# Four and four: the order of the high and low matmuls inside a chunk of a split fp32 projection

## What is computed

```python
proj = jnp.einsum("bsd,de->bse", h, w_in[l])
...
x = x + gate1[:, None, :] * jnp.einsum("bsd,de->bse", merged, w_out[l])
...
ff = jnp.square(jax.nn.relu(jnp.einsum("bsd,df->bsf", h2, w_ff1[l])))
x = x + gate2[:, None, :] * jnp.einsum("bsf,fd->bsd", ff, w_ff2[l])
...
h = jnp.einsum('bsd,dn->bsn', x, w_in)
```

## Time and profile before

| | |
|---|---|
| median of 3 runs | 2717.64 us (2717.5 to 2718.73) |
| span of the profiled execution | 2715.6 us |
| PE busy in it | 2667.7 us, 98% |
| PE weight loads busy | 2305.3 us, 85% |
| DVE busy | 1945.2 us, 72% |
| ACT busy | 1379.7 us, 51% |
| POOL busy | 145.2 us, 5% |

### The profile page before, as it was taken

The page is one execution under the profiler, slowest core; times in us unless marked ns, Lnnn a source line. Parts: engine busy times, 40 slices in busy tenths (PEclk is TensorE's granted clock), DMA queues, the critical chain, the costliest instruction groups (busy, mean ns, idle before and its releaser), DMA issues.

```text
span 2715.6 us, 38672 instructions
## 1 busy us (share of the span) xinstructions
PE 2667.7 (98%) x15098; PEld 2305.3 (85%) x15098; DVE 1945.2 (72%) x2837; ACT 1379.7 (51%) x2049; POOL 145.2 (5%) x179
## 2 busy tenths in 40 slices
PE   7999999999999999999999999999999999999997
PEld 6788788888888888888888888878888888888886
DVE  7776888887898876666666676666566766665666
ACT  2158666554544655445544445545554455445643
POOL 0000000000001000000000010100001121000002
PEclk9999999999999999999999999999999999999998
DMA  9964777778888675665565555665545556655453
GB/s 390 409 224 146 260 238 255 272 270 300 292 321 319 230 243 185 191 190 187 187 193 187 179 182 181 191 181 178 156 160 185 187 181 191 185 181 161 147 173 115
DMA packets 162533, 583.98 MB, mean 215 GB/s; under 512 B 19088, under 2 KB 20368, under 8 KB 162352
## 3 DMA queue, kind: packets, MB, share of 16 engines
q1 hardware_dynamic: 157248, 567.71, 62.3%
q0 software_dynamic: 4528, 12.43, 1.7%
q10 hardware_dynamic: 576, 1.37, 0.1%
HBM read 574.05 MB, written 2.15 MB: 212 GB/s over the span
## 4 chain that ended last, share of the span: by engine, by line
PE 86%; DVE 7%; DMA 3%; ACT 2%; issue 1%; SPq 0%; ACTq 0%; DVEq 0%
PE bank L794 49%; PE bank L802 25%; PE bank L755 3%; DVE both_w L1463 2%; DMA raw<-in_w_x 2%; PE pO L851 1%; PE pS L828 1%; PE bank L760 1%; DMA raw<-in_ada 1%; PE bank L740 1%; ACT both_w L1058 1%; PE pT L840 1%; DVE XC L1926 1%; PE bank L772 1%; PE pS L897 1%
## 5 line engine op out<-in xcount | busy, mean ns | idle before, releaser
L1463 DVE TENSOR_TENSOR both_w<-raw,both_w 128x1024 fp32r<-128x1024 f32 x848 | 1036.7, 1234 | 453.1 <-ACT both_w L1058 448.4
L1058 ACT ACTIVATE both_w<-raw 128x1024 fp32r<-128x1024 f32 x848 | 878.1, 1048 | 517.6 <-PE bank L802 458.3
L794 PE MATMUL bank<-H,both_w 128*128 128x512 f32 x4000 | 1015.7, 396 | 2.6 <-ACT both_w L1058 1.2
L794 PEld LDWEIGHTS bank<-H,both_w 128*128 128x128 f32 x4000 | 721.1, 189 | 144.5 <-issue 6.3
L802 PEld LDWEIGHTS bank<-H,both_w 128*128 128x128 f32 x4000 | 545.5, 190 | 40.7 <-DVE both_w L1463 1.3
L802 PE MATMUL bank<-H,both_w 128*128 128x256 f32 x4000 | 557.5, 282 | 0.9 <-DVE both_w L1463 0.9
L794 PE MATMUL bank<-F,both_w 128*128 128x512 f32 x1024 | 256.4, 392 | 0.0
L1503 DVE SCALAR_TENSOR_TENSOR raw<-raw,CR 128x1024 f32<-128x1024 f32 x192 | 232.5, 1217 | 18.3 <-DMA raw<-in_ada 17.0
L794 PEld LDWEIGHTS bank<-F,both_w 128*128 128x128 f32 x1024 | 184.2, 189 | 32.8
L802 PEld LDWEIGHTS bank<-F,both_w 128*128 128x128 f32 x1024 | 139.7, 190 | 10.0
L802 PE MATMUL bank<-F,both_w 128*128 128x256 f32 x1024 | 142.8, 282 | 0.0
(11 more groups left out here) (293 smaller groups left out, 2523.3 us busy)
## 6 DMA issues: line engine op xcount, KB each, us to landing
raw<-in_w_in SPq DMA_DIRECT2D x360, 512.0 KB, 3.9
raw<-in_w_ff SPq DMA_DIRECT2D x256, 512.0 KB, 3.9
raw<-in_ada SPq DMA_DIRECT2D x192, 512.0 KB, 5.2
raw<-in_w_out SPq DMA_DIRECT2D x96, 512.0 KB, 4.5
raw<-in_w_vw SPq DMA_DIRECT2D x48, 512.0 KB, 3.7
raw<-in_w_x SPq DMA_DIRECT2D x32, 512.0 KB, 15.7
raw<-in_w_lru_out SPq DMA_DIRECT2D x32, 512.0 KB, 4.8
raw<-in_w_attn_out SPq DMA_DIRECT2D x32, 512.0 KB, 5.0
```

Source lines behind the costliest of these rows:

```text
L794: pe.matmul(out[i].rearrange("p (a s) -> p a s", a=2), whi[:, s, at_:at_ + 128], both[:, :, kt, :], start=(c == 0 and k == 0), stop=False, ...
L1058: act.activation(whi[:, s, 0:el.n], raw[el.slot][:, 0:el.n], ACT.Copy).then_inc(s_hi, 1)
L1463: dve.tensor_tensor(wlo[:, s, 0:n], raw[el.slot][:, 0:n], v32(whi[:, s, 0:n]), ALU.subtract).then_inc(s_lo, 1)
```

## The change

In `products_wide` the loop over k is cut in two halves of two k each. Each half does its four wide matmuls and then its four narrow ones: a chunk is 4 wide, 4 narrow, 4 wide, 4 narrow, where it was 8 wide, 8 narrow. The number of matmuls and weight loads, their shapes, the banks, the two waits for the weights and the one signal at the end are as before. The wait for `s_lo` now stands before the fifth matmul of the chunk instead of before the ninth. The sum in a bank is taken in another order. No other function is touched.

```diff
-            for k in range(4):
-                kt = 4 * un.corder[c] + k
...
-            pe.wait_ge(s_lo, split_no[order[ch]])
...
-            for k in range(4):
-                kt = 4 * un.corder[c] + k
...
+            for pair_ in range(2):
+                for k in (2 * pair_, 2 * pair_ + 1):
+                    kt = 4 * un.corder[c] + k
...
+                        pe.matmul(out[i].rearrange("p (a s) -> p a s", a=2), whi[:, s, at_:at_ + 128], both[:, :, kt, :],
+                                  start=(c == 0 and k == 0), stop=False, skip_group_check=True)
+                if pair_ == 0:
+                    pe.wait_ge(s_lo, split_no[order[ch]])
+                for k in (2 * pair_, 2 * pair_ + 1):
+                    kt = 4 * un.corder[c] + k
...
+                        ins = pe.matmul(out[i][:, high], wlo[:, s, at_:at_ + 128], xh[:, kt, :], start=False,
+                                        stop=(c == un.nkc - 1 and k == 3), skip_group_check=True)
```

More of the change, by code:

```diff
@@ L783, in products_wide @@
             out = [banks[un.bank + i] for i in range(2)]
+            high = slice(256, 512) if un.x in ("Y0", "Y1") else slice(0, 256)
             pe.wait_ge(s_hi, split_no[order[ch]])
-            for k in range(4):
-                kt = 4 * un.corder[c] + k
[L787 to L795, removed]
@@ L796, in products_wide @@
-            pe.wait_ge(s_lo, split_no[order[ch]])
-            high = slice(256, 512) if un.x in ("Y0", "Y1") else slice(0, 256)
-            for k in range(4):
-                kt = 4 * un.corder[c] + k
[L800 to L803, removed]
+            for pair_ in range(2):
+                for k in (2 * pair_, 2 * pair_ + 1):
+                    kt = 4 * un.corder[c] + k
+                    if begins[un.x] is un:
+                        pe.wait_ge(*ready[un.x](kt))
+                    elif un.kind == "q" and un.j == 0:
+                        pe.wait_ge(*ready["H1"](kt))
+                    for i in range(2):
+                        at_ = k * 256 + i * 128
+                        pe.matmul(out[i].rearrange("p (a s) -> p a s", a=2), whi[:, s, at_:at_ + 128], both[:, :, kt, :],
[4 more added lines that the diff above has]
+                    kt = 4 * un.corder[c] + k
+                    for i in range(2):
+                        at_ = k * 256 + i * 128
+                        ins = pe.matmul(out[i][:, high], wlo[:, s, at_:at_ + 128], xh[:, kt, :], start=False,
+                                        stop=(c == un.nkc - 1 and k == 3), skip_group_check=True)
```

## The result

| | before | changed |
|---|---|---|
| median, 12 runs each | 2717.39 us | 2722.57 us |
| ratio, 95% interval | | 1.002 (1.0012 to 1.0027) |
| span of the profiled execution | 2715.6 us | 2720.4 us |

What follows compares the result with a forecast made beforehand. PE's pace was taken to bound the kernel. The order added +9.0 us, low-weight wait and fresh activations were entered as 0: span 2724.6 us, plus 2 us between span and median, 2726.6 us; range 2710 to 2734.

Steps and rivals of the forecast that it cites:

- slower: Whole kernel: measured time over 2723.1 us, about 0.2% (5.4 us) above no change; chance 0.60.
- What bounds the kernel: Whole kernel: PE, busy 98% of the span, sets the pace; only its waits and matmul distances can matter.
- The order of wide and narrow: PE's 772 chunks: two full wide-narrow turns instead of one add 11.7 ns a chunk, +9.0 us.
- The wait for the low weights: PE's wait for DVE's low split, four wide matmuls earlier: two chunks lack enough lead, +0.5 to +1.8 us.
- Fresh activations: Two PE standstills, 906.77 and 1646.36: four narrow matmuls fill the idle time, -0.9 us together.
- The reason under the main term: PE's chunks: four narrow matmuls unsettle wide ones as much as eight, since narrow ones settle after two; supports +9.0 us.
- Never settled: PE's chunks: wide matmuls stay unsettled, narrow ones partly offset it; +5 ns a chunk, +4 us, 2722 us; chance 0.12.
- Whole price per turn: PE's chunks: the second turn costs the whole 20 ns; +15.4 us, 2733 us; chance 0.11.
- Faster: PE's chunks: unsettling goes by the number of narrow matmuls just before, so four cost less; 2707 to 2711 us; chance 0.18.
- No change: PE's chunks: two half turns cost one; 2717.6 us, give or take 2; chance 0.15.
- The rule named beside it: PE's matmul distances: N/2.4 + 2.5 ns from column count alone, without memory; 2600 ns a chunk in either order.

Runs made afterwards that it cites:

- wait alone: Kernel before, eight wide and eight narrow kept, only the low-weight wait moved ahead of the fifth wide matmul; 2717.76 us against 2717.27, ratio 1.0002.
- 6, 2, 2, 6: Kernel before with each chunk reordered to 6 wide, 2 narrow, 2 wide, 6 narrow; 2717.45 us in one execution against 2717.35.
- rotated: Kernel before with each chunk reordered to 4 wide, 8 narrow, 4 wide, low-weight wait before the narrow ones; 2717.65 us against 2717.27, ratio 1.0001.
- two and two: Kernel before with each chunk reordered to 2 wide, 2 narrow, four times; 2711.75 us against 2717.27, ratio 0.9981.
- 2, 2, 6, 6: Kernel before with each chunk reordered to 2 wide, 2 narrow, 6 wide, 6 narrow; 2708.62 us against 2717.15, ratio 0.997.
- one and one: Kernel before with wide and narrow matmuls alternating one by one; 2732.15 us against 2715.75, ratio 1.0059.
- sixteen: Kernel before with narrow matmuls first in every second chunk, so runs are sixteen long; 2709.77 us against 2717.27, ratio 0.9975.
- fourteen and two: Kernel before with two chunks together reading 8 wide, 14 narrow, 2 wide, 2 narrow, 6 wide; 2706.93 us against 2717.15, ratio 0.9965.
- thirty-two: Kernel before with two chunks worked together, runs 32 long in units of four chunks, 16 in units of two; 2826.33 us against 2717.35, ratio 1.0403.
- all wide: Changed kernel's order, but low-weight matmuls stream both activation halves, 512 columns, leaving no narrow matmul in these units; 3349.46 us in one execution.

## Why the prediction was right, and where it was off

The sign held, and 2722.6 us lies in the range, 4.0 us under the forecast of 2726.6. The size falls at the edge: 5.2 us is just under the bound of 5.4 that I had set for "slower", to which I gave 0.60.

*What bounds the kernel.* Held. The wait alone cost nothing, PE's distances made the difference, and DVE, ACT and the releases kept their times.

*The order of wide and narrow*, forecast +9.0 us. This term was over. In the feed-forward stretch 2805 ns were forecast and 2806.7 measured. The four parts were 930 + 472.5 twice; they came as 928 + 478 and 930 + 471. The step that failed is the multiplication by 772. In a chunk that stands right behind other work (attention pieces, gates), the wide matmuls are unsettled already before the change, as the 1.98 us of the earlier trace rows could have told me, and there the second turn adds nothing: between 313 and 613 us, 28 such chunks take 2905 ns each before and 2905 in the changed kernel, while those with no other work beside them go from 2793 to 2803. In some of these stretches the changed kernel also falls into another rhythm, 230, 231, 236, 228 | 117, 118, 120, 120 in every half, which makes 2800 ns a chunk instead of 2807. From chunk 50 to the end, less the two filled gaps, the difference grows by 4.85 + 1.91 + 0.47 + 0.60 = 7.8 us. With the step of 0.54 us near 2194, which belongs to the next term, taken off, 7.3 us are left, and some 0.2 from the chunks ahead of 50. So the term was over by some 1.5 us.

*The wait for the low weights*, forecast +0.5 to +1.8, in two chunks. This held: PE's waits for it went from 0.9 to 1.9 us, and the difference steps up by 0.36 us behind 287 us and by 0.54 us near 2194.

*What was in none of my terms.* Between chunks 46 and 50 the difference fell by 2.05 us. The wait at 300 us, for DVE to take over the scores before, was 0.54 us shorter, and the clock did not fall behind it, which gave the other 1.5 us. Whether the clock falls there went with the length of that standstill in nine traces. By the distance between the last matmul before it and the first behind it: 2.65 us (before), 2.63 (6, 2, 2, 6), 2.14 (rotated) and 2.14 (wait alone), and the mean clock in the window 300.5 to 304 was 0.54, 0.75, 0.57 and 0.61; 2.11 us (the changed kernel), 1.73 (two and two), 1.72 (2, 2, 6, 6), 1.49 (one and one) and 1.19 (sixteen), and it was 1.00.

Elsewhere the length alone does not decide. Near 287 us PE waited 1.85 us in fourteen and two and 1.84 us in sixteen, and the mean clock from 287.6 to 291.2 us was 0.53 in the first and 1.00 in the second. Two waits of PE in the kernel with runs of thirty-two, and its window view around them (granted clock third from the end):

```profile
1706.73 0.63 PE L862 MATMUL pT<-cst,LP 128*128 128x128 f32 x4 [2.93 <-ACT LP L1151]
...
1725.59 0.63 PE L862 MATMUL pT<-cst,LP 128*128 128x128 f32 x4 [2.04 <-ACT LP L1151]
```

```profile
1703.00:1713.00 10.00, 7.07 (x39) 5.89 (x38) 4.59 (x7) 4.72 (x12) 1.99 (x4) 1.00 0.43 131
1724.00:1731.00 7.00, 5.41 (x19) 4.42 (x20) 2.60 (x5) 4.10 (x10) 1.96 (x4) 0.76 0.57 152
```

Behind the longer standstill the clock stayed, behind the shorter it fell. No run changed a standstill alone, so what tips the clock stays open.

*Fresh activations*, forecast -0.9. The gaps gave -0.47 and -0.60.

The remaining -0.44 us stands before the first chunk of this form and has nothing to do with the change. Sum: -0.44 + 0.58 - 2.05 - 1.07 + 7.8 = 4.8 us.

*The reason under the main term* was only half right. I took the state after four narrow matmuls to be that after eight because the narrow ones settle after two. For a run that meets wide matmuls at the end of their slow stretch this stands: even two narrow ones start it again (6, 2, 2, 6). But in the order of the change no narrow run meets settled ones, and there is no single state: in turn 235, 233, 236, 224 and 233, 236, 228, 233. That the sum came out right within 2 ns is partly luck; the same reasoning gave 2801 for both 2, 2, 6, 6 and 6, 2, 2, 6, and the first was off by 21.

*The rivals.* "Never settled" was the nearest in time (2722) and describes the state rightly, but it gave +5 ns where 13.3 came. "Whole price per turn" is refuted by the changed kernel itself (13.3 ns for the second turn, not 20) and by two and two. "Faster", through the number of narrow matmuls just before, is wrong for four, though two of them well placed do make the kernel faster. "No change" fell with the changed kernel's 2806.7 ns. The rule named beside it (the Trainium skill, "TensorE: Matmul & The Clock Gate", "Back-to-back issue gap") takes the distance from the column count alone, and the section gives that formula for a single isolated matmul. By it all nine paces of the table would be one number, and they run from 2777.8 to 2826.6. It fits in kind only where all lengths are equal, in the kernel without narrow matmuls, and even there 226.6 ns stand against its 216.

What is not explained is the mechanism. Shown is that the surplus of the feed-forward stretch needs two lengths beside each other, that it does not come from waits or from the switch of weights, and that it depends on the sequence over half a dozen matmuls. The slow stretch itself is not bound to a change of length: in the kernel before, behind a short wait near 2189.5 us between matmuls of 512 columns on both sides, the starts stand 337, 236, 228, 233, 231, 226 and then 227 ns apart, the same sequence. So it looks like the recovery from a break in the rhythm, of which a change of length is one kind. In the feed-forward stretch of the kernels looked at (before, the change, one and one, two and two, 2, 2, 6, 6, 6, 2, 2, 6 and all wide) each weight load starts 1 to 6 ns behind the start of the matmul before its own, so loads and matmuls move in one rhythm, and the traces do not tell which of them holds up the other, nor what keeps the memory.

## What to carry to other kernels

Where PE is busy all the time, read the distance between the starts of matmuls, by their place in the row, and compare with a stretch in which neighbours are alike: here 20 ns of 2793 were hidden there, 15 us over the 772 chunks, where all of PE's waits came to 27. In this kernel matmuls of unlike length paid least in long runs, as far as waits elsewhere allowed them (thirty-two lost 109 us to them and to the clock), or where a run of two was placed right after the first two of the wide ones; runs of four were the worst of the even splits tried except one by one. Before summing an effect over all chunks, sort the chunks by what stands before them.

## What the runs showed of the hardware that I had not expected

The order of fp32r matmuls of 512 and 256 columns changes their pace by up to 49 ns a chunk (2826.6 against 2777.8 ns, 1.8%) with no wait anywhere, and not steadily with the number of turns: 32, 16, 8, 4, 2 and 1 in a run give 2778, 2784, 2793, 2807, 2787 and 2827 ns. Among their like they settle at 226.6 and 120 ns, each with its own weight load. After 2.38 us of standstill at 300 us the granted clock was at its lower level for most of 3.5 us, which cost six matmuls 200 ns each; after 1.84 us, in the changed kernel, it was not, but elsewhere it fell after 1.85 and stayed after 2.93. A spell of that kind costs 1.5 us, as much as some hundred of the change's second turns, and shows in the page's 40 slices not at all.
